# A second issuing queue for the expert weights: down tiles from ACT, gate and up tiles from SP

## The reference

```python
for gi in range(N_GROUPS):
    hid = jax.nn.silu(jnp.einsum('td,edf->tef', x, w_gate[gi])) * jnp.einsum('td,edf->tef', x, w_up[gi])
    y = y + jnp.einsum('tef,efd->td', hid * dense_w[:, gi, :, None], w_down[gi])
```

## Time and profile before

| | us |
|---|---|
| median of 3 runs | 1163.35 (1162.99 to 1165.38) |
| the profiled execution | 1163.8 |
| its span, first to last instruction | 1162.0 |
| PE busy | 1011.3 (87% of the span) |
| DVE, ACT, POOL busy | 349.9, 220.8, 85.5 |
| mean granted TensorE clock | 0.941 of full speed |
| moved by DMA | 343.81 MB, mean 296 GB/s |
| of it by SP's queue q1 | 287.97 MB |
| of it by ACT's queue q10 | 2.10 MB |

### The profile page before, as it was taken

One profiled execution on the slowest core, in us unless ns is written; L12 is line 12 of the kernel. 1 busy time (PEld: TensorE's weight loads), 2 busy tenths in 40 slices (PEclk: granted clock), 3 DMA queues, 4 the chain that ended last, 5 costly groups with the idle time before them and its releaser, 6 DMA issues.

```text
span 1162.0 us, 15987 instructions
## 1 busy us (share of the span) xinstructions
PE 1011.3 (87%) x6782; PEld 730.0 (63%) x6782; DVE 349.9 (30%) x668; ACT 220.8 (19%) x468; POOL 85.5 (7%) x107
## 2 busy tenths in 40 slices
PE   7999999999999999979999999877758767677665
PEld 6888888778877777768888665444434434344323
DVE  3304483377213233336211121211162111111113
ACT  2112114103422231343000031110101011111102
POOL 0002121000132323100000000000000000000000
PEclk9999999999999999989999979997887898988888
DMA  9974467594659879845345949999999999999991
GB/s 317 284 253 147 151 208 256 167 291 115 228 203 308 302 275 319 297 169 173 131 145 213 383 188 417 416 416 418 417 418 416 417 417 416 416 417 416 417 410 70
DMA packets 138921, 343.81 MB, mean 296 GB/s; under 512 B 7736, under 2 KB 91960, under 8 KB 122456
## 3 DMA queue, kind: packets, MB, share of 16 engines
q1 hardware_dynamic: 123232, 287.97, 66.1%
q0 software_dynamic: 14464, 52.68, 12.8%
q10 hardware_dynamic: 1152, 2.10, 0.5%
HBM read 320.49 MB, written 22.20 MB: 295 GB/s over the span
## 4 chain that ended last, share of the span: by engine, by line
PE 66%; SPq 13%; DMA 13%; DVE 5%; issue 2%; ACT 1%; POOL 0%; DVEq 0%; ACTq 0%; POOLq 0%
PE psum L937 37%; SPq L778 13%; DMA arena<-in_w_up 12%; PE psum L694 4%; PE psum L677 4%; PE psum L704 3%; PE psum L986 3%; PE psum L946 2%; PE psum L998 2%; PE psum L1207 1%; PE psum L1142 1%; PE psum L1130 1%; DVE arena L1639 1%; PE psum L1121 1%; PE psum L1081 1%
## 5 line engine op out<-in xcount | busy, mean ns | idle before, releaser
L937 PE MATMUL psum<-arena 128*128 128x264 f32 x2048 | 474.1, 388 | 0.0
L937 PEld LDWEIGHTS psum<-arena 128*128 128x128 f32 x2048 | 386.4, 191 | 79.6 <-issue 16.1
L694 PE MATMUL psum<-arena 128*32 128x256 f32 x2048 | 142.9, 430 | 76.7 <-DMA arena<-in_w_up 76.5
L694 PEld LDWEIGHTS psum<-arena 128*32 128x32 f32 x2048 | 77.1, 123 | 139.1 <-issue 114.0
L1278 ACT ACTIVATE arena<-psum 128x264 f32<-128x264 f32 (+3 forms) x148 | 61.7, 427 | 335.4 <-PE psum L937 261.4
L704 PE MATMUL psum<-arena 128*32 128x256 f32 x1024 | 75.7, 446 | 11.7 <-ACT arena L1496 11.7
L677 PE MATMUL psum<-arena 128*128 128x128 f32 (+1 forms) x384 | 78.5, 336 | 1.0 <-DVE arena L1880 1.0
L677 PEld LDWEIGHTS psum<-arena 128*128 128x128 f32 (+1 forms) x384 | 58.8, 210 | 28.5 <-issue 17.6
L1278 ACT ACTIVATE arena<-arena 128x1024 f32<-128x1024 f32 (+6 forms) x62 | 55.0, 918 | 105.2 <-DVE arena L1794 87.8
L1747 DVE SCALAR_TENSOR_TENSOR arena<-arena 128x512 f32<-128x512 f32 x64 | 43.8, 747 | 91.6 <-ACT arena L1278 91.5
L1939 DVE SCALAR_TENSOR_TENSOR arena<-arena,psum 128x128 f32<-128x128 f32 x32 | 9.2, 288 | 201.9 <-ACT arena L1482 201.9
(11 more groups left out here) (240 smaller groups left out, 720.5 us busy)
## 6 DMA issues: line engine op xcount, KB each, us to landing
arena<-in_w_gate SPq DMA_DIRECT2D x64, 1024.0 KB, 23.1
arena<-in_w_up SPq DMA_DIRECT2D x64, 1024.0 KB, 23.0
arena<-in_w_down SPq DMA_DIRECT2D x64, 1024.0 KB, 23.1
arena<-in_w_in SPq DMA_DIRECT2D x48, 1024.0 KB, 5.4
arena<-in_state_ret POOLq DMA_DIRECT2D x16, 1024.0 KB, 7.3
out_ret_s<-arena POOLq DMA_DIRECT2D x16, 1024.0 KB, 7.5
arena<-in_w_mem_kv SPq DMA_DIRECT2D x8, 1024.0 KB, 11.4
arena<-in_cache_mem_k POOLq DMA_DIRECT2D x8, 1024.0 KB, 5.9
```

Source lines behind the costliest of these rows:

```text
L694: mm = pe.matmul(psum[32 * a:32 * a + SLOTS, bank, 0:256], tokens[:, 4 * half + k, SLOTS * j:SLOTS * (j + 1)], w[:, :, k, P * a:P * (a + 1 ...
L937: mm = pe.matmul(ps(task)[:, 0:T], w[:, k, (i % 2) * P:(i % 2 + 1) * P], rhs[:, k, :], start=k == 0, stop=k == KT - 1 and not two)
```

## The change

The down parts of experts 3 to 31 are no longer issued by SP. ACT issues both, behind its wait for `y_full` of the expert three back and ahead of the two copies that already followed that wait; they go through ACT's own queue. SP's loop runs over parts 0 to 3 alone. The helpers that name a part's source and place move out of SP's function, so that both can use them. The first three experts (18 transfers at L771) stay with SP; tiles, semaphores and PE's, DVE's and POOL's programs stay the same.

```diff
-            part_used = (gate_up_half, gate_up_half, gate_up_full, gate_up_full, down_half, y_full)
+            part_used = (gate_up_half, gate_up_half, gate_up_full, gate_up_full)
             for e in range(3, EXPERTS):
-                for i in range(PARTS):
+                for i in range(4):
                     s = tile_at(e, i)
                     sp.wait_ge(part_used[i], e - 2)
                     sp.dma_start(into(s, i), expert_part(e, i)).then_inc(chunk_loaded[s], 16)
...
                 act.wait_ge(y_full, e + 1)
                 if q >= 2:
                     act.wait_ge(scatter_full, 8 * (q - 1))
+                if e + 3 < EXPERTS:
+
+                    for i in (4, 5):
+                        s = tile_at(e + 3, i)
+                        act.dma_start(into(s, i), expert_part(e + 3, i)).then_inc(chunk_loaded[s], 16)
                 low_rows(q % 2, j, 3 + e % 2)
```

More of the change, by code:

```diff
@@ L713, in last_scatter_bank, with expert_part, into @@
             return (7, 5, 6, 0)[d % 4]
+        wg = dram["w_gate"].rearrange("g e (h p j) f -> (g e) h p (j f)", h=2, p=P)
+        wu = dram["w_up"].rearrange("g e (h p j) f -> (g e) h p (j f)", h=2, p=P)
+        wd = dram["w_down"].rearrange("g e (k p) d -> (g e) p k d", p=P)
+        def expert_part(e, i):
+            if i < 4:
+                return (wg, wu)[i % 2][bass.ds(e, 1), i // 2].rearrange("a p x -> p (a x)")
+            lo = 2 * (i - 4)
+            return wd[bass.ds(e, 1), :, lo:lo + 2, :].rearrange("a p k f -> p (a k) f")
+        def into(s, i):
+            return slot[:, s, :] if i < 4 else slot[:, s, :].rearrange("p (k n) -> p k n", k=2)
         block = ctx.enter_context(nc.Block())
@@ L747, in _ @@
                     chunk_loaded[n % RING1], 16)
[L749 to L761, removed]
             sp.wait_ge(ret_ready, VT)
```

## The result

The changed kernel takes 1168.73 us (median of 6 runs, 1168.47 to 1169.94), the kernel before 1163.3 us in the same comparison (1161.69 to 1165.43). The ratio is 1.0046, with a 95% interval of 1.0033 to 1.0059: slower by about 5 us. The prediction was 1168.0. The profiled execution took 1168.47 us, its span is 1166.6 us; the sum had these at 1168.4 and 1166.6.

The account below looks back on a forecast made before the run. The expert stage was taken as bound by a fixed-length transfer at 417 GB/s. Issue and start terms of 0 plus 4.6 us for landing order gave 1163.35 + 4.6 = 1168.0 us; 8-in-10 range 1162.0 to 1174.0.

Parts of the forecast that it names:

- the sum: Whole kernel: span 1162.0 + 0 + 0 + 4.6 = 1166.6 us; the execution 1.8 us above its span, so 1168.4.
- The bound: Expert stage: a transfer of fixed length, 174 tiles at 2.51 us each, 437.5 us at 417 GB/s.
- SP's loss of 58 issues, worth 0: Expert stage: over 120 us of SP's issuing time saved, but spent before a full queue; nobody waits for SP.
- ACT's gain of 58 issues, worth 0: Expert stage: 0.338 us an issue, 0.7 us per expert, hidden in ACT's 6.0 us wait before each tanh.
- The start, worth 0: Expert 3, from about 694 us: down tiles issued about 1 us later, under 10 us of gate and up transfer.
- The order of landing, +4.6: Stage end: expert 31's last gate and up tiles land at about 1138.0 instead of 1133.5, moving everything behind them 4.6 us.
- Theory P: Long-run experiment, DMA queues: engines alternate pieces, so 4 KB beside 8 KB gets a third; the early backlog never drains.
- The forecast that no down product would wait for a tile: Sign at PE's down products: none waits for a DMA; PE's last landing wait ends at about 1138.
- The second queue does not raise the rate: Rival, DMA from 694 to 1138 us: a second queue raises the rate; at 425 GB/s 1159.8 us; 18%.
- Transfers did not land in the order of issue: Rival, DMA queues: transfers still land in issue order, down tiles stay last, time stays at 1163.4 us; 11%.
- PE did not become the bound: Rival, last two or three experts: PE at the lower clock is 3.4 us too slow per expert, about 1175 to 1178; 11%.
- ACT was not held up: Rival, ACT's issues: they meet SP's full queue; at 10.5 us a pair 20 us more, 1188; 5%.

Follow-up runs that it names:

- the third experiment: Changed kernel with expert 31's two down tiles given back to SP at the end of its stream, ACT issuing the other 56: 1162.89 us, ratio 0.9995.

## Why the prediction was right

**The bound** (a transfer of fixed length from 694 to 1138 us): right, 416 against 417 GB/s, with the last tile landed at 1138.0.

**SP's loss of 58 issues, worth 0**: right. SP's time in issues fell from 401 to 268 us and its waits for PE rose from 76 to 167, and nothing came of either.

**ACT's gain of 58 issues, worth 0**: right in the time, as the run with 56 of them shows. The size was 0.45 us an issue instead of 0.34, 0.9 per expert. ACT is not held up by SP's full queue: its longest issue took 2.8 us, SP's 9.0. Four of ACT's 58 took over 1 us, all between 736 and 795 us, when its own queue was longest.

**The start, worth 0**: right, by the same run.

**The order of landing, +4.6**: right in mechanism and size. The last second half moved by 4.57 us, and three runs tie that to the order of expert 31's six tiles: the order alone gives the loss on one queue, two moved transfers give it, and giving back two removes it. That the size was met to 0.03 us is luck: with the same tiles last, the second half started at 1138.14, 1138.52 and 1137.67 in three profiled executions, which is +4.1 to +5.0.

**What was off** lies inside that step and did not reach the sum. The prediction let the engines share between the queues evenly, or a third for ACT, and had down tiles land 10 to 15 us after issue; they took 27.6, and gate and up tiles 38.7 instead of about 30. A third was the case (34.4% of the bytes), and a third is just what down tiles need on average, 2 of 6 tiles. At one tile in 7.5 us, 27.6 us is a queue of 3.7 tiles instead of two. The trace shows where this backlog came from. ACT issued its first six pairs of down tiles 8.1 to 13.1 us apart (at 698.4, 708.7, 716.8, 726.1, 735.9 and 749.1), since PE ran through the first experts that fast, while the transfer needs 15.1 us for an expert. The first pair landed after 12.7 and 19.5 us; for the four pairs issued from 740 to 800 and for the last four pairs the source view of L1505 has:

```profile
DMA to landing us min/median/max: 30.5/36.3/42.2
```

```profile
DMA to landing us min/median/max: 13.0/19.9/26.7
```

So the backlog did shrink, slowly, and Theory P is wrong in that part; a share a little over a third fits this, but was not tried. With equal pieces on both sides ACT's share is half while both queues hold work, and the landing fell to 13.8 us. The prediction also had expert 31's down tiles land some 20 us before the end; it was 16 and 9 us. The Trainium skill, DMA: Bandwidth & Descriptors, section "Queues, rings and completion order", has each engine alternate between its queues packet by packet. The trace agrees in so far as the two queues moved 13169 and 13050 of the profile's packets; the page's packet is a group of several descriptors, each for one piece, and how many are taken at one turn no run here shows. The forecast that no down product would wait for a tile was wrong by one wait of 1.2 us, at 747.91, when the backlog was near its height.

**The rivals.** The second queue does not raise the rate: 416 with, 417 without, and 421 in either case with long runs. Transfers did not land in the order of issue: expert 31's down tiles were issued from 1103.56 on, after its last up tile (1102.1), and landed 16 and 9 us before it. PE did not become the bound, but in the profiled execution it came within 0.15 us of it, so the case of a late PE was missed narrowly. ACT was not held up. The Trainium skill, DMA: Bandwidth & Descriptors, section "Issuing engines are not separate DMA queues", which speaks against the change, agrees with the trace: the rate was 416 GB/s with two queues and 417 with one, what was saved was issuing time, and no one had been waiting for it.

## What to carry to other kernels

Where a stage is one long transfer at a constant rate, moving transfers to another queue need not shorten it; here it only decided what lands last. Look at the last landing and at the work that hangs on it: the tiles with the least work behind them belong at the end, and two transfers in 174 can carry the whole effect of a change. If such a stage is to get faster, look at the length of the contiguous runs before looking at the queues.

## What was not expected of the hardware

The length of the runs matters above 4 KB too: 8 KB runs in the down tiles gave 421 instead of 417 GB/s, and 4 KB runs everywhere 409.

How much one queue holds is not a number of bytes. With SP the only issuer, the median landing was 18.8 us with 4 KB runs everywhere (first line), 23.1 with a third of them, and 27.4 with none (second line; DMA issues, median us to landing last):

```profile
arena<-in_w_up SPq DMA_DIRECT2D x64, 1024.0 KB, 18.8
```

```profile
arena<-in_w_up SPq DMA_DIRECT2D x64, 1024.0 KB, 27.4
```

At 409 and 421 GB/s these are 7.3 and 11.0 tiles under way. In the last case SP waited 147 us for PE (102.2 + 44.6), about twice as long as before, so the wait for free places may be what limits it, and the depth itself stays open.

Part of the spread may lie in the final norm. Two profiled executions, of two kernels that are alike from there on, differ by 1.7 us in it: its 16 products took 5.52 us in the kernel before and 3.83 in the third experiment, with the granted clock at 0.50 (the 1.2 GHz level) and at 1.00 (2.4 GHz) from 1150 to 1152; ahead of both PE had been idle for about 3 us. Timeline of each:

```profile
1148.10 5.52 PE L1269 MATMUL psum<-arena 128*128 128x264 f32 x16 [3.27 <-issue]
```

```profile
1148.09 3.83 PE L1269 MATMUL psum<-arena 128*128 128x264 f32 x16 [3.00 <-issue]
```

Why PE was granted one level or the other there was not tried, nor whether it accounts for the whole spread, which is 5 us. It is why the end of the last down product, and not the span, was compared wherever a microsecond mattered. The profiled executions of the kernel before and of the changed kernel both have 5.52 us there, so their spans can be compared.
